# One-hots of a dense scatter moved to ScalarE, value rows respread over the periods, and one expert group instead of two gathered whole

## The chip, the cores and the metric

One core of one Trainium2 chip runs the program. The metric is device time in microseconds for one execution. The kernel before was timed in three runs: median 2061.11, lowest 2057.94, highest 2066.78. A profiled execution is another run, with its own time.

## What is computed

A decoder layer over 256 tokens of width 2048: a mixer (causal pooling and forgetting attention), memory cross-attention, and a product-key expert network. Only the last part matters here. `h` is (256, 2048), heads are 8, keys 128, and 16384 experts have a row `u` and a row `v` of 2048 floats each:

```python
q = (h @ w_query).reshape(B, S, PEER_HEADS, 2, PEER_HALF)
scores = jnp.einsum('bshcd,hckd->bshck', q, sub_keys)
s_top, i_top = lax.top_k(scores, 16)
cand = s_top[..., 0, :, None] + s_top[..., 1, None, :]
cand_idx = i_top[..., 0, :, None] * 128 + i_top[..., 1, None, :]
best, pos = lax.top_k(cand.reshape(..., 256), 16)
expert_idx = take_along_axis(cand_idx.reshape(..., 256), pos)
gate = softmax(best)
act = gelu(einsum('ckd,cd->ck', expert_u[expert_idx], h))
out = einsum('ck,ckd->cd', gate * act, expert_v[expert_idx])
```

Each token picks 16 experts in each of 8 heads, so 128 rows of u and 128 of v. The layer ends with the residual sum and an RMS norm.

## The kernel before, in words

Tokens are two tiles of 128 (c = 0, 1), one token in each partition. A group is one head of one tile: 16 groups, g = 8c + head, each with 16 expert columns k. One gather brings one row for each of the 128 tokens of a tile.

**Routing** (VectorE: `route_keys`, `route_pairs`, `route_experts`, L1165 to L1189) writes the expert numbers `idx` of a group and adds 1 to the semaphore `routed`. `gate_exp` (ScalarE, L723) and `gates` (VectorE, L1194) make its softmax. Group g + 2 is routed inside the period of group g.

**Dots** (VectorE, `dot_products`, L1236 and L1238): two halves of 1024 elements for each u row. The u rows land in seven slots: four in `u_ring`, two in `u_mid`, one in `u_high`; for groups 0 and 1 only the four. GpSimd issues all gathers in one written order (`gather_u` L495, `gather_v` L502): within period p for each k first u row (p, k), which waits until the dot that used its slot is done, then a share of the value rows, each of which waits until TensorE has used its slot (`v_used`). After 16 dots, `sum_dots` (L1200), gelu on ScalarE (L751), and `weights` (L1206, L1207), behind the first two dots of the next group.

**Values** of tile 0: for each of 128 expert columns ScalarE writes a diagonal matrix of weights (`diagonals`, L731, four buffers) and TensorE multiplies it with the value row tile, four matmuls of 512 columns into `misc` (`take_values`, L1664). `v_share(p)` says which of the 128 are taken in period p: 8 in each of periods 2 to 7, 10 in each of 8 to 15.

**Dense part.** Experts whose first key is 80 or more (48 of 128 keys) are not gathered as value rows: such indices lie beyond the gather's bound and are skipped, and their weight in the diagonal is set to zero. Their weights are scattered instead into a matrix wT (128 second keys x 48 first keys x 128 tokens), and after the dots TensorE multiplies 48 tiles of 128 consecutive v rows with it (`dense_tile`, L1697, each tile once for tile 0 into `misc` and once for tile 1 into `acc`). SyncE loads the tiles into three slots of `u_ring` (L432). The last WHOLE = 2 groups (14 and 15) are left out of this: their value rows are gathered whole. The scatter runs by batches of 8 tokens, 16 batches for each tile. `turn_lists` (TensorE, L1682) turns the lists of a tile over, `take_lists` (VectorE, L1214) copies them to `listsT`. For each batch VectorE compares to get `hotA` (second key one-hot, 128 x 8 x 128, L1221) and `hotB` (first key one-hot of 48, L1223, times the weight, L1225); TensorE multiplies them per token (`scatter_weights`, L1691); ScalarE copies the result into wT (`weights_T`, L745). `hotA`, `hotB` and the result have two buffers. `scatters(p)` says which batches go into period p: three in 8 to 12, one in 13, for tile 0; eight in 14 and eight in 15 for tile 1. TensorE and ScalarE go through a period in ten steps, a value and then its batches; VectorE has the batches in front of dots 2 to 15.

**Late values** of tile 1: 128 more gathers into seven slots (`late_landed`); VectorE adds them weighted into `y_sum` (`add_values`, L1270, 2048 elements), except that of the last 16 every second goes to TensorE (`late_diagonal` L738, `take_late` L1673). `finish(0)` stands on VectorE before addition 112 and waits for the low half of the dense tiles; `finish(1)` (L1279 to L1292) ends the program.

The start of the layer takes the first 740 us and is not touched. The periods run from about 812 (the end of group 0's dots) to 1666, dense tiles and late values from there to the end.

```python
for p in range(1, GROUPS):
    pool.wait_ge(routed, p + 1)
    share = v_share(p)
    for k in range(TOP):
        gather_u(p, k)
        for n in share[k * len(share) // TOP:(k + 1) * len(share) // TOP]:
            ...
            gather_v(n, n % VS, v_landed[n % VS])
```

## Time and profile before

| | |
|---|---|
| median of three runs | 2061.11 us |
| the profiled execution's own time | 2061.64 us |
| its span | 2059.6 us |
| mean granted TensorE clock | 0.952 of full speed |
| TensorE matmul busy | 1773.1 us (86%) |
| VectorE busy | 1402.9 us (68%) |
| ScalarE busy | 447.8 us (22%) |
| GpSimd busy | 1027.9 us (50%) |
| HBM read | 729.91 MB |

The shares are means over stages with different limits: in the first 740 us TensorE is nearly always busy, in the periods DMA and VectorE are. So the page is only the start, and the trace is asked by stretches of time. A busy figure for GpSimd here is the time it takes to issue gathers. PEclk is the clock granted to TensorE as a share of 2.4 GHz; 0.5 is its lower level, 1.2 GHz.

### The profile page before, as it was taken

How to read it: one execution, taken by the hardware profiler on the slowest of the kernel's cores; microseconds unless marked ns; L12 is line 12 of the kernel's file. 1: busy time of each engine (PE TensorE's matmuls, PEld its weight loads, DVE VectorE, ACT ScalarE, POOL GpSimd, SP SyncE). 2: the span in 40 equal slices, each digit the busy share in tenths (PEclk: the TensorE clock that was granted, in tenths of full speed). 3: DMA queues.
4: the chain of work that ended last, by engine and by line, in shares of the span. 5: the costliest groups of instructions: out<-in, count | busy, mean ns of one | idle time of the engine just before them, and what ended most of it. 6: DMA issues, size and time to landing. Idle time of an engine off the chain costs nothing.

```text
span 2059.6 us, 21224 instructions
## 1 busy us (share of the span) xinstructions
PE 1773.1 (86%) x7539; PEld 1184.9 (58%) x7539; DVE 1402.9 (68%) x2235; ACT 447.8 (22%) x720; POOL 1027.9 (50%) x643
## 2 busy tenths in 40 slices
PE   7999999999999999466565667877778899999996
PEld 7998998888998898322222223333334544444442
DVE  4382453233333258899888888999989877887865
ACT  5344453345434410201101101111101100000001
POOL 4443343444332313456556546554556756776742
PEclk9999999999999999789999889988889999999999
DMA  8975455655535689899999999999999989999997
GB/s 207 245 172 137 152 181 159 196 191 185 165 122 190 198 313 396 316 408 420 420 419 419 414 390 388 401 389 393 394 419 402 377 323 403 387 405 371 395 421 290
DMA packets 157648, 647.40 MB, mean 314 GB/s; under 512 B 25894, under 2 KB 31086, under 8 KB 95598
## 3 DMA queue, kind: packets, MB, share of 16 engines
q0 software_dynamic: 73728, 450.98, 54.2%
q1 hardware_dynamic: 83824, 195.16, 29.5%
q8 instruction: 58, 0.95, 0.2%
q14 instruction: 38, 0.31, 0.0%
HBM read 729.91 MB, written 2.10 MB: 355 GB/s over the span
## 4 chain that ended last, share of the span: by engine, by line
PE 47%; DMA 19%; DVE 18%; issue 8%; POOL 6%; ACT 1%; DVEq 0%; SPq 0%; POOLq 0%; ACTq 0%
PE misc L1664 10%; DMA u_ring<-in_peer_u_dram,idx 7%; DMA v_low<-in_peer_v_dram,idx 6%; DVE product L1236 6%; DVE product L1238 5%; PE acc L1355 5%; PE acc L1357 5%; PE acc L1356 5%; PE acc L1362 5%; PE acc L1363 5%; PE acc L1364 5%; PE acc L1691 2%; DMA v_more<-in_peer_v_dram,idx 2%; DMA v_last<-in_peer_v_dram,idx 2%; DMA v_high<-in_peer_v_dram,idx 2%
## 5 line engine op out<-in xcount | busy, mean ns | idle before, releaser
L455 POOL TENSOR_TENSOR w_lo<-raw,w_hi 128x1024 fp32r<-128x1024 f32 x112 | 273.7, 2444 | 428.9 <-ACT w_hi L543 428.6
L1664 PE MATMUL misc<-v_low,diag 128*128 128x512 f32 x512 | 263.5, 667 | 132.7 <-ACT diag L731 87.9
L1664 PE MATMUL misc<-v_high,diag 128*128 128x512 f32 x512 | 263.2, 666 | 108.4 <-DMA v_high<-in_peer_v_dram,idx 71.4
L834 DVE TENSOR_TENSOR w_lo<-raw,w_hi 128x1024 fp32r<-128x1024 f32 x112 | 150.1, 1341 | 267.6 <-ACT w_hi L543 267.3
L543 ACT ACTIVATE w_hi<-raw 128x1024 fp32r<-128x1024 f32 x224 | 237.0, 1060 | 352.4 <-PE acc L1364 169.2
L495 POOL DMA_INDIRECT u_ring<-in_peer_u_dram,idx x160 | 207.3, 1296 | 202.2 <-DVE dots L1238 139.6
L1664 PEld LDWEIGHTS misc<-v_low,diag 128*128 128x128 f32 x512 | 105.7, 214 | 278.2 <-issue 207.3
L1355 PE MATMUL acc<-t_hi,w_hi 128*128 128x256 f32 x896 | 255.3, 285 | 0.0
L1357 PE MATMUL acc<-t_hi,w_lo 128*128 128x256 f32 x896 | 253.5, 283 | 0.0
L1356 PE MATMUL acc<-t_lo,w_hi 128*128 128x256 f32 x896 | 253.5, 283 | 0.0
L1664 PEld LDWEIGHTS misc<-v_high,diag 128*128 128x128 f32 x512 | 104.6, 212 | 253.6 <-issue 157.2
L1236 DVE CUSTOM_DVE_ANT_0 product<-u_ring,hn 128x1024 bf16<-128x1024 f32 x160 | 196.0, 1225 | 51.9 <-DMA u_ring<-in_peer_u_dram,idx 36.0
L502 POOL DMA_INDIRECT v_low<-in_peer_v_dram,idx x102 | 156.5, 1535 | 135.1 <-PE misc L1664 74.7
L502 POOL DMA_INDIRECT v_high<-in_peer_v_dram,idx x100 | 152.0, 1520 | 122.1 <-PE misc L1664 85.4
L1238 DVE CUSTOM_DVE_ANT_0 product<-u_ring,hn 128x1024 bf16<-128x1024 f32 x160 | 195.7, 1223 | 0.0
L1697 PE MATMUL misc<-u_ring,wT 128*128 128x512 f32 x384 | 174.4, 598 | 4.1 <-DMA u_ring<-in_peer_v_dram 3.5
L1362 PE MATMUL acc<-w_hi,t_hi 128*128 128x512 f32 x448 | 177.3, 396 | 0.0
L1364 PE MATMUL acc<-w_hi,t_lo 128*128 128x512 f32 x448 | 174.5, 389 | 0.0
L1363 PE MATMUL acc<-w_lo,t_hi 128*128 128x512 f32 x448 | 174.4, 389 | 0.0
L1697 PE MATMUL acc<-u_ring,wT 128*128 128x512 f32 x384 | 172.3, 592 | 0.0
L1355 PEld LDWEIGHTS acc<-t_hi,w_hi 128*128 128x128 f32 x896 | 171.9, 192 | 0.2
L1356 PEld LDWEIGHTS acc<-t_lo,w_hi 128*128 128x128 f32 x896 | 171.9, 192 | 0.1
(248 smaller groups left out, 2571.9 us busy)
## 6 DMA issues: line engine op xcount, KB each, us to landing
u_ring<-in_peer_v_dram SPq DMA_DIRECT2D x48, 1024.0 KB, 8.9
raw<-in_w_in_dram SPq DMA_DIRECT2D x64, 512.0 KB, 5.1
raw<-in_xattn_wk_dram SPq DMA_DIRECT2D x32, 512.0 KB, 4.6
raw<-in_xattn_wv_dram SPq DMA_DIRECT2D x32, 512.0 KB, 4.0
raw<-in_w_out_dram SPq DMA_DIRECT2D x32, 512.0 KB, 4.6
raw<-in_xattn_wq_dram SPq DMA_DIRECT2D x32, 512.0 KB, 4.6
raw<-in_xattn_wo_dram SPq DMA_DIRECT2D x32, 512.0 KB, 4.8
praw<-in_peer_wq_dram SPq DMA_DIRECT2D x32, 512.0 KB, 8.5
```

The lines of the kernel that those rows point to most:

```text
L455: nc.gpsimd.tensor_tensor(w_lo[:, j % RING, :, :], raw[:, j % RING, :, :], w_hi[:, j % RING, :, :].bitcast(F32), ALU.subtract).then_inc(lo ...
L502: nc.gpsimd.indirect_dma_start(out=v_slot(slot), out_offset=None, in_=v_rows, in_offset=bass.IndirectOffsetOnAxis(ap=idx[:, n // TOP, n % ...
L1236: nc.vector.tensor_tensor_reduce(out=product[:, 0:D // 2], in0=u_slot(n)[:, 0:D // 2], in1=hn[:, c, 0:D // 2], scale=1.0, scalar=0.0, op0= ...
L1238: nc.vector.tensor_tensor_reduce(out=product[:, D // 2:], in0=u_slot(n)[:, D // 2:], in1=hn[:, c, D // 2:], scale=1.0, scalar=0.0, op0=ALU ...
L1355: nc.tensor.matmul(o, wh, hi[:, kt, :], start=first and ct % 2 == 0, stop=False, skip_group_check=True)
L1356: nc.tensor.matmul(o, wh, lo[:, kt, :], start=False, stop=False, skip_group_check=True)
L1357: ins = nc.tensor.matmul(o, wl, hi[:, kt, :], start=False, stop=last and ct % 2 == 1, skip_group_check=True)
L1362: nc.tensor.matmul(o, xh, w_hi[:, s, kk, :], start=first, stop=False)
L1363: nc.tensor.matmul(o, xh, w_lo[:, s, kk, :], start=False, stop=False)
L1364: ins = nc.tensor.matmul(o, xl, w_hi[:, s, kk, :], start=False, stop=last)
L1664: ins = nc.tensor.matmul(o, diag[:, n % 4, :], v_slot(n % VS)[:, i * CW:(i + 1) * CW], start=False, stop=False)
L1697: ins = nc.tensor.matmul(o, wT[c][:, t, :], u_ring[:, t % 3, i * CW:(i + 1) * CW], start=c == 1 and t == 0, stop=c == 0 and t == DENSE - 1)
```

## The change

WHOLE becomes 1, so group 14 takes part in the dense scatter too and only group 15 is gathered whole; all 16 batches of tile 1 then stand in period 15, since group 14's weights are known only there. Twelve of them (and all sixteen of tile 0) get `hotA` from ScalarE: the square of (second key - column) for 8 tokens in turn, then one relu of 1 - 2x over all; every fourth batch of tile 1 (b % 4 == 3) keeps VectorE's comparison. `hotB` stays on VectorE. Value rows are taken 4 in period 1, 6 in each of periods 2 to 7, 11 in each of 8 to 15. Batches of tile 0 stand at k = 8, 11 and 14. TensorE and ScalarE walk a period in 16 steps, as VectorE does. Routing is one period ahead instead of two. The u slots from group 2 on begin with the three outside `u_ring`, the late value slots with the three outside v_low and v_high. `weights(15)` stands behind three late additions.

```diff
-    WHOLE = 2
+    WHOLE = 1
...
-            return n % 4 if n < 2 * TOP else (n - 2 * TOP) % 7
+            return n % 4 if n < 2 * TOP else (n - 2 * TOP + 4) % 7
...
-        def scatters(p):
+        def scatters(p, k):
+            if p < PH or k < 2:
+                return range(0)
+            if p < GROUPS - WHOLE:
+                b = 3 * (p - PH) + (k - 8) // 3
+                return range(b, b + 1) if k in (8, 11, 14) and b < BATCHES else range(0)
+            return range(BATCHES + (k - 2) * BATCHES // 14, BATCHES + (k - 1) * BATCHES // 14)
+        def by_dve(b):
+            return b >= BATCHES and b % 4 == 3
...
+        FIRST_V = 4
         def v_share(p):
             if p < 2:
-                return range(0)
-            return range(8 * (p - 2), 8 * (p - 1)) if p < PH else range(48 + 10 * (p - PH), 58 + 10 * (p - PH))
+                return range(0, FIRST_V * p)
+            if p < PH:
+                return range(FIRST_V + 6 * (p - 2), FIRST_V + 6 * (p - 1))
+            at = FIRST_V + 6 * (PH - 2) + 11 * (p - PH)
+            return range(at, min(at + 11, TILE0))
+        def taken(p, k):
+            n = len(v_share(p))
+            return n if k >= TOP else sum(TOP * i + n < k * n for i in range(n))
+        def late_slot(m):
+            return (m + 4) % V2S
...
+            def key_one_hots(b):
+                t, q, rows = b % BATCHES * WB, b % 2, HS if b < BATCHES else HS - WHOLE * TOP
+                act.wait_ge(lists_copied, b // BATCHES + 1)
+                if b >= 2:
+                    act.wait_ge(wT_done, b - 1)
+                for i in range(WB):
+                    ins = nc.scalar.activation(hotA[0:rows, q, i, :], keys[0:rows, :], ACT.Square, scale=-1.0,
+                                               bias=listsT[0:rows, 1, t + i:t + i + 1])
+                ins.then_inc(key_squares, 1)
+                act.wait_ge(key_squares, act_batches(b + 1))
+                nc.scalar.activation(hotA[0:rows, q, :, :], hotA[0:rows, q, :, :], ACT.Relu, scale=-2.0, bias=1.0).then_inc(key_hot, 1)
...
             def period(p):
...
+                for k in range(TOP):
+                    diagonals(share[taken(p, k):taken(p, k + 1)])
+                    if k == 2 and p in (PH, GROUPS - WHOLE):
+                        key_one_hots(0 if p == PH else BATCHES)
+                    if k == 5 and p + 1 < GROUPS:
+                        gate_exp(p + 1)
+                    for b in scatters(p, k):
+                        if (b + 1) % BATCHES and not by_dve(b + 1):
+                            key_one_hots(b + 1)
                         weights_T(b)
                 gelu(p, p % 2, p // PH)
...
                 dve.wait_ge(lists_done, c + 1)
+                if c:
+                    dve.wait_ge(key_hot, BATCHES)
+                    dve.wait_ge(hot_ready, BATCHES)
...
             def one_hots(b):
+                dve.wait_ge(lists_copied, b // BATCHES + 1)
+                if by_dve(b):
+                    nc.vector.tensor_tensor(hotA[0:rows, q, :, :], ...)
...
             def period(g):
                 dot_products(g, q, c, range(0, 2))
                 weights(g - 1)
-                    route_keys(g + 2)
+                    route_keys(g + 1)
                 for k in range(2, TOP):
+                    for b in scatters(g, k):
                         one_hots(b)
                     dot_products(g, q, c, range(k, k + 1))
+                    if k == 3 and more:
+                        route_pairs(g + 1)
                     if k == 5 and more:
+                        route_experts(g + 1)
+                    if k == 9 and more:
+                        gates(g + 1)
                 sum_dots(g, q)
...
-            dot_products(1, 1, 0, range(8, AHEAD))
+            dot_products(1, 1, 0, range(8, 9))
             dve.wait_ge(scores_ready, 2)
-            route(2)
+            route_keys(2)
+            dot_products(1, 1, 0, range(9, 11))
+            route_pairs(2)
+            dot_products(1, 1, 0, range(11, 13))
+            route_experts(2)
+            dot_products(1, 1, 0, range(13, 15))
             gates(2)
-            dot_products(1, 1, 0, range(AHEAD, TOP))
+            dot_products(1, 1, 0, range(15, TOP))
             sum_dots(1, 1)
-            route(3)
-            gates(3)
...
-            weights(GROUPS - 1)
             for m in range(TILE0):
+                if m == 3:
+                    weights(GROUPS - 1)
...
             def scatter_weights(b):
                 pe.wait_ge(hot_ready, b + 1)
+                if not by_dve(b):
+                    pe.wait_ge(key_hot, act_batches(b + 1))
...
+            for n in v_share(1):
+                take_values(n)
             for p in range(2, GROUPS):
...
+                for k in range(TOP):
+                    for n in share[taken(p, k):taken(p, k + 1)]:
                         take_values(n)
+                    for b in scatters(p, k):
                         scatter_weights(b)
```

GpSimd's issue order changes in the same way: after the u rows of group 1 it issues the four values of `v_share(1)`, then goes on as before with `late_slot`.

## Rows read from the trace of the kernel before

**Rows 1.** Windows by period: busy us (instructions), granted clock, DMA share, GB/s

```profile
926.40:976.70 50.30, 32.18 (x64) 13.10 (x64) 46.77 (x102) 5.61 (x13) 30.91 (x25) 0.90 1.02 420
976.70:1194.20 217.50, 131.01 (x250) 50.37 (x250) 187.22 (x410) 22.76 (x52) 125.89 (x97) 0.93 1.01 418
1194.20:1542.30 348.10, 270.14 (x724) 129.03 (x723) 315.46 (x661) 42.95 (x104) 181.72 (x154) 0.88 0.98 396
1542.30:1603.10 60.80, 52.42 (x192) 30.13 (x191) 55.80 (x93) 7.63 (x18) 43.56 (x25) 0.89 1.00 402
1603.10:1666.10 63.00, 55.12 (x216) 32.21 (x214) 55.25 (x92) 7.01 (x19) 37.54 (x23) 0.95 0.96 383
1666.10:1999.60 333.50, 328.41 (x784) 146.89 (x783) 257.86 (x113) 3.53 (x8) 227.80 (x114) 0.99 0.97 385
```

**Rows 2.** The DMA queues: packets, MB, share of 16 engines

```profile
q0 software_dynamic: 73728, 450.98, 54.2%
```

**Rows 3.** Timeline of VectorE: start, us, instruction

```profile
865.74 0.17 DVE L1200 TENSOR_TENSOR dot_sums<-dots 128x16 f32<-128x16 f32 x1
...
876.15 1.23 DVE L1236 CUSTOM_DVE_ANT_0 product<-u_ring,hn 128x1024 bf16<-128x1024 f32 x1
...
999.25 1.23 DVE L1236 CUSTOM_DVE_ANT_0 product<-u_ring,hn 128x1024 bf16<-128x1024 f32 x1 [0.26 <-DVE pos L1160]
...
1001.77 1.23 DVE L1236 CUSTOM_DVE_ANT_0 product<-u_mid,hn 128x1024 bf16<-128x1024 f32 x1
```

**Rows 4.** Groups of instructions, 1200 to 1680: busy, mean ns, idle before

```profile
L1221 DVE TENSOR_TENSOR hotA<-listsT,keys 128x1024 f32<-128x1024 f32 x16 | 19.5, 1221 | 0.7
...
L1223 DVE TENSOR_TENSOR hotB<-listsT,keys 128x384 f32<-128x384 f32 x16 | 8.8, 550 | 0.0
```

**Rows 5.** The window from 860, and TensorE's first values in its timeline

```profile
860.00:880.00 20.00, 6.00 (x8) 2.59 (x9) 17.86 (x53) 3.16 (x8) 11.26 (x11) 0.52 0.95 373
...
874.00 6.32 PE L1664 MATMUL misc<-v_low,diag 128*128 128x512 f32 x8 [28.88 <-ACT diag L731]
```

**Rows 6.** Groups of ScalarE, whole run (busy, mean ns, idle before), and its timeline

```profile
L543 ACT ACTIVATE w_hi<-raw 128x1024 fp32r<-128x1024 f32 x224 | 237.0, 1060 | 352.4 <-PE acc L1364 169.2 <-PE acc L1357 159.9 <-DMA raw<-in_w_in_dram 15.3
...
L751 ACT ACT_TABLE_LOAD x14 | 18.0, 1283 | 0.2
...
L768 ACT ACTIVATE junk<-y_sum 128x512 bf16<-128x512 f32 x8 | 4.9, 618 | 349.8 <-DVE y_sum L1279 329.6 <-DVE y_sum L1281 20.2
...
1492.13 1.26 ACT L731 ACTIVATE diag<-ident,low_wts 128x128 f32<-128x128 f32 x4
```

**Rows 7.** Timeline of TensorE, then of ScalarE: one step of period 14

```profile
1562.57 3.67 PE L1664 MATMUL misc<-v_high,diag 128*128 128x512 f32 x8 [0.96 <-ACT diag L731]
...
1568.92 5.31 PE L1664 MATMUL misc<-v_high,diag 128*128 128x512 f32 x8 [0.96 <-ACT diag L731]
...
1567.99 0.49 ACT L745 ACTIVATE wT<-acc 128x384 f32<-128x384 f32 x1 [5.57 <-PE acc L1691]
1568.38 0.39 ACT L731 ACTIVATE diag<-ident,low_wts 128x128 f32<-128x128 f32 x1
```

**Rows 8.** Timeline of TensorE: first and last dense tiles

```profile
1674.60 3.70 PE L1697 MATMUL misc<-u_ring,wT 128*128 128x512 f32 x8 [0.58 <-ACT wT L745]
...
1994.28 5.40 PE L1697 MATMUL misc<-u_ring,wT 128*128 128x512 f32 x8 [3.55 <-DMA u_ring<-in_peer_v_dram]
```

**Rows 9.** Timeline of TensorE, then of VectorE: the tail

```profile
2045.57 3.70 PE L1673 MATMUL acc<-v_low,diag 128*128 128x512 f32 x8 [1.21 <-DMA v_low<-in_peer_v_dram,idx]
...
2049.38 2.48 DVE L1281 TENSOR_TENSOR y_sum<-acc,y_sum 128x512 f32<-128x512 f32 x4 [3.94 <-PE acc L1673]
```

**Rows 10.** Timeline of VectorE, then waits from 1542 to 1680

```profile
1550.81 0.56 DVE L1214 COPY listsT<-acc 96x384 f32<-96x384 f32 x1 [0.97 <-PE acc L1682]
...
1674.77 0.17 DVE L1206 TENSOR_TENSOR lists<-acts,gate 128x16 f32<-128x16 f32 x1 [8.53 <-ACT acts L751]
...
POOL v_low L502 <- PE misc L1664: 20.6, 5, 8.1
```

More of the change, by code:

```diff
@@ L298, in hybrid_layer @@
         PC = CH * ITEMS["peer"][1]
-        AHEAD = 12
         TILE0 = PH * TOP
@@ L490, in gather_u @@
                 before = u_before(n)
-                if before is None:
+                if before is not None:
+                    pool.wait_ge(dot_done, before + 1)
+                elif n >= 2 * TOP:
                     pool.wait_ge(scores_ready, ITEMS["peer"][1])
-                elif before >= 0:
-                    pool.wait_ge(dot_done, before + 1)
                 nc.gpsimd.indirect_dma_start(
@@ L511, in _, with first_values @@
                 gather_u(0, k)
-            for p in range(1, GROUPS):
+            def first_values(n):
+                if n >= VS:
+                    pool.wait_ge(v_used, n - VS + 1)
+                elif n == 2:
+                    pool.wait_ge(peer_used, PC - CH)
+                gather_v(n, n % VS, v_landed[n % VS])
+            pool.wait_ge(routed, 2)
+            for k in range(TOP):
+                gather_u(1, k)
+            for n in v_share(1):
+                first_values(n)
+            for p in range(2, GROUPS):
                 pool.wait_ge(routed, p + 1)
@@ L753, in period @@
             def period(p):
-                share, turns = v_share(p), scatters(p)
-                for i in range(10):
-                    diagonals(share[i:i + 1])
-                    if i == 3 and p + 2 < GROUPS:
-                        gate_exp(p + 2)
-                    for b in turns[i * len(turns) // 10:(i + 1) * len(turns) // 10]:
+                share = v_share(p)
+                for k in range(TOP):
[7 more added lines that the diff above has]
+                            key_one_hots(b + 1)
                         weights_T(b)
@@ L1701, in _ @@
                 nc.tensor.matmul(o, zeros[:, 0:P], zeros[:, :], start=True, stop=False)
+            for n in v_share(1):
+                take_values(n)
             for p in range(2, GROUPS):
-                share, turns = v_share(p), scatters(p)
+                share = v_share(p)
                 if p == PH:
@@ L1707, in _ @@
                     turn_lists(1)
-                for i in range(10):
-                    for n in share[i:i + 1]:
+                for k in range(TOP):
+                    for n in share[taken(p, k):taken(p, k + 1)]:
                         take_values(n)
-                    for b in turns[i * len(turns) // 10:(i + 1) * len(turns) // 10]:
+                    for b in scatters(p, k):
                         scatter_weights(b)
```

61 lines of the change are left out of this document (22 added, 39 removed).

## The prediction

> **What bounds the kernel now.** Read the windows by period first, a period being the dots of one of the 16 groups [rows 1]. The DMA share is 1.02 in period 3 and 1.01 in periods 4 to 7, at 420 and 418 GB/s, and 0.98 at 396 GB/s in periods 8 to 13. The queues [rows 2] tell how much a gather moves. One whole gather is 128 rows of 8 KB, 1.0486 MB; the indirect queue moved 450.98 MB, which is 430.1 of them. 256 are u rows and 32 are whole value rows (groups 14 and 15), so the other 224 value gathers, whose high keys are skipped, are worth 142.1, or 0.634 each. The sum below uses that.
>
> Then VectorE. A dot comes every 2.52 us (999.25 to 1001.77), 40.4 us in a group [rows 3]. Period 3 (50.3 us, DMA fed it) shows dots and one routing with nothing else: VectorE's floor without one-hots is 50.3. A batch of one-hots adds hotA 1.22 and hotB twice 0.55 [rows 4], so periods 8 to 13 with three batches have a VectorE floor of 50.3 + 3 x 2.32 = 57.3; they take 348.1 / 6 = 58.0 [rows 1]. Their bytes are 16 + 10 x 0.634 = 22.3 gathers, 23.4 MB, 55.8 us at 0.419 MB per us. So VectorE bounds these. Periods 3 to 7 need (16 + 8 x 0.634) x 1.0486 / 0.419 = 52.7 us for bytes and take (50.3 + 217.5) / 5 = 53.6: DMA bounds them.
>
> After the last dot, TensorE bounds. The 48 dense tiles start at 1674.60, when the last batch's copy is in, and the low half of the sums is complete with the record of 1994.28, at about 1999.5. That stretch of 325 holds 93 half tiles, one DMA wait of 3.55 and one record 1.8 longer than its like: 319.6 / 93 = 3.44 us for a half tile, without gaps [rows 8]. DMA is at 0.97 beside that [rows 1]: it is nearly a second bound. In the tail TensorE waits for each late value row (1.21 for the last), its sums are taken up at 2049.38, and the output is done 10.2 later [rows 9].
>
> **The change, part by part.**
> (1) Start of period 2. Before, groups 2 and 3 are both routed before it: group 1's dots are summed at 865.74, and the first dot of group 2 starts at 876.15 [rows 3]. After, group 3 is routed inside period 2. The same work moves, it doesn't vanish; what vanishes is the 10.3 us between them in which no dot runs, and four early values and gathers into three free slots use the DMA there. The first u gather of group 2 goes out behind 13 of group 1's dots and the routing, three dots or 7.6 us before the period starts; two u rows and the four values, 4.5 gathers or 11 us of DMA, were issued in the six us before it. So I let the first dot wait some 2 us: 868. Period 2 then ends at 868 + 50.3 + 1 = 919.3 against 926.4: -7.
> (2) Periods 3 to 7 carry 6 values, not 8: 19.8 gathers, 20.8 MB, 49.6 us. VectorE's 50.3 takes over. With half a us of jitter 50.8 each: 5 x (50.8 - 53.6) = -14.
> (3) Periods 8 to 14. In 8 to 12 three hotA leave VectorE (-3.66, floor 53.6); 13 has one batch, 14 none. Eleven values make 22.97 gathers, 24.1 MB, 57.4 us. DMA is the bound in all seven; at 57.8 each 404.6 against 348.1 + 60.8 = 408.9: -4. The value rows that periods 2 to 7 no longer carry are paid here. All 128 still land before the end of period 15, so no bytes are saved up to there.
> So group 15's dots start at 1603.1 - 25 = 1578.
> (4) Period 15 is where the change pays. Its sixteen batches were eight, beside ten values; now eleven values. ScalarE makes twelve wide one-hots: eight squares of 128 columns and a relu over 1024. Neither is in the trace. The diagonal has the same shape and a column operand: 0.39, four in 1.26, so eight take 0.39 + 7 x 0.29 = 2.4; a pass over 1024 takes 1.06 at w_hi [rows 6]. Called K: 2.4 + 1.06 + two handovers of 0.1 = 3.7. Ends: 3.5 with nothing between, 6.1 if a square and a relu each cost a table load of 1.28 ([rows 6]; the squares of L768 need none behind a sqrt).
> The Trainium skill, page "ScalarE: Activation LUTs", section "Rules for kernel authors", says to put relu, add and multiply on VectorE, which speaks against this move. Instruction by instruction the rows agree, 1.22 against about 3.7. Whether that shows hangs on the chain that follows (rival F takes it as it stands).
> That chain runs through TensorE and ScalarE in program order. TensorE does value (3.67), batch (6.35 - 3.67 - 0.95 = 1.73); ScalarE copies the batch (0.39 until it takes the next, 0.49 until done), makes the next diagonal (0.39), and TensorE starts again 0.95 after the batch: 1562.57, 1568.92, a step of 6.35 [rows 7]. The new order puts the next batch's K ahead of this batch's copy. With a value between batches K hides beside it (3.7 against 5.4). Where two batches follow one another without a value, ScalarE stands: copy 0.5, K 3.7, copy 0.5, diagonal and handover 0.4: 5.1 instead of 0.95. From the loop bounds: values at k = 1, 2, 3, 5, 6, 8, 9, 11, 12, 14, 15; batches one at each k from 2 to 15, two at 8 and at 15. From the copied lists on: TensorE's second value and the first batch, with two K on ScalarE beside them (7.4), 8.4; nine value+batch, 9 x 5.4 = 48.6; handovers 4 x 0.95 + one double without K 2.7 + 4 x 5.1 = 26.9; last batch and copy 2.3. Sum 86. The granted clock is 0.88 to 0.95 in periods 8 to 15 [rows 1], and a value at the low level costs 5.31 instead of 3.67 [rows 7]: +5. The lists are copied 8 us after the period's start (1542.3 to 1551.4 in period 14, with a gelu wait of 1.3 that goes [rows 10]). Together 8 + 86 + 5 = 99; dense tiles start at 1578 + 99 = 1677, +2.5 against now. VectorE has 40.4 + 16 x 1.10 + 4 x 1.22 = 63 to do and waits for TensorE; DMA needs 57 and idles. What four periods' rearrangement won is given back in one.
> (5) Dense tiles. Group 14's value rows shrink by 16 x 0.366 x 1.0486 = 6.1 MB, 16 us at the 385 GB/s of that stretch [rows 1]. TensorE's 320 stays, and the stall of 3.55 plus 1.8 goes: end of the low half at 1677 + 320 = 1997 (-2.6).
> (6) Tail. All seven slots can hold landed rows when the low half ends, so the eight late values go at TensorE's pace: three high tiles 10.3, then 8 x 3.6, 39 us, against 49.8 (1999.5 to 2049.3 [rows 9]): -10.7. The queue still gives the last two gathers 33 to 36 us after the low half, inside 39. Behind it 10.3 as now.
> (7) weights(15) moves behind three additions: VectorE's 8.53 us wait [rows 10] is filled. VectorE has 112 x 2.46 = 276 us of additions under TensorE's 320, so this costs or gives nothing while that cover holds.
> Sum on the profiled execution: 1997 + 39 + 10.3 = 2046.3 in a span of 2059.6, -13.3; I take -11, since (3) and (4) have more ways to lose a microsecond than to win one. Its own time is 2061.64, the median of the three runs 2061.11: **2050**.
>
> **The rivals.**
> A, forecast: (1) to (6) as they stand, -18 to -6. Chance 0.42.
> B, period 15 is shorter: K overlaps more than I let it, or fewer slow stretches. If the four doubles cost 2.7 as the one without K does, 10 us go, without the +5 of the clock 15, and some more from (3) if DMA holds 420. End -20 to -35, 2027 to 2042. For it: ScalarE is busy for only 43 us of 348 in periods 8 to 13 [rows 1]. Against: order, not load, makes those waits. Chance 0.2.
> C, slower: TensorE's clock in period 15. When TensorE waits, the granted clock falls to its lower level: 0.52 from 860 to 880 behind 28.88 us of idleness [rows 5], and eight records took 6.32, not 3.67. Period 15 has nine waits, TensorE busy some 75%. If the clock is low for more than half of the stretch, each value costs 2.65 and each batch 1.7 more: 11 x 2.65 + 16 x 1.7 = 56 in full; at 60% 34, of which 5 is counted: end -11 + 29 = +18, 2080. It decides from a mean clock of about 0.75 in period 15 on. Against it: 0.95 in the same mixture now. With it goes K at its upper end, 4 x 2.4 = 10 in the doubles and some beside values, about +5 in the end. Chance 0.15.
> D, the periods give nothing: ScalarE's and TensorE's order stalls POOL, as TensorE's values hold it back now (20.6 us for v_low alone, 1542 to 1680) [rows 10], and u gathers queue behind it. Periods 8 to 14 then take 59.5, +12 against (3): end 2062. Chance 0.12.
> E, the smaller gathers do not show, because dense tiles and tail are TensorE's already: (5) and (6) give nothing; +2.5 of (4) alone, 2064. Against it: the waits for DMA in rows 9. Chance 0.06.
> F, K is hidden nowhere: all twelve lengthen period 15 by 3.7 - 1.22 = 2.5, 30 us, where the chain above counts 4 x (5.1 - 0.95) = 17. End +13 on the forecast, 2063. Against it: in the step of 6.35 ScalarE works 0.9 and waits 5.57 [rows 7]. The skill's rule named in (4) would have it so. Chance 0.05.
>
> **Numbers.** A measurement of this kernel tells 0.5%, 10.3 us, from no change: faster is below 2050.8. A lies 0.24 below and 0.18 above that, B below; D, E and F inside but for 0.02 of D that stalls more; C above 2071.4. Faster 0.44, same 0.39, slower 0.17. Range: B without its last few us (0.06 left out) to C's near end (0.12 left out), 2030 to 2074.
>
> **What would show it.** Period 2 starts before 870; periods 3 to 7 at 50.5 to 51.5; 8 to 14 at 57 to 58.5 with DMA at 1.0; group 15's dots start at 1573 to 1585; period 15 lasts about 90 with DMA share near 0.7; K at 3.5 to 3.8 with no table load; dense tiles start within 5 us of 1677, without a DMA wait; TensorE's late values back to back. Wrong if period 15's chain lasts under 80 or over 105, or if dense tiles wait for DMA.

## The result and the profile after

The changed kernel takes **2075.0 us** (median of 6 runs, 2072.25 to 2077.07) against 2060.45 for the kernel before (6 runs): ratio 1.0069, interval 1.0056 to 1.0083. It is slower by 0.7%, where the prediction had 2050 and faster. Its profiled execution has a span of 2070.2 us at a mean granted clock of 0.947; it is the fastest of the six, so the profiles below differ by 10.6 us where the medians differ by 14.5.

Windows of the changed kernel, columns as in [rows 1]: periods 3 to 7 with half of 2, periods 8 to 13, period 14, period 15, the dense tiles to the end of the low half, the tail.

```profile
919.00:1173.30 254.30, 145.07 (x242) 56.21 (x241) 233.93 (x510) 25.13 (x55) 150.00 (x112) 0.83 1.01 416
1173.30:1526.90 353.60, 285.94 (x786) 134.58 (x785) 297.04 (x645) 101.74 (x256) 187.55 (x160) 0.94 1.00 406
1526.90:1588.10 61.20, 44.97 (x90) 18.07 (x89) 46.82 (x104) 7.09 (x16) 32.43 (x28) 0.92 1.00 405
1588.10:1689.10 101.00, 79.71 (x325) 48.28 (x324) 59.98 (x105) 50.69 (x134) 24.15 (x21) 0.86 0.61 233
1693.50:2017.90 324.40, 322.48 (x745) 142.84 (x746) 263.62 (x114) 2.36 (x5) 245.35 (x116) 0.99 0.99 389
2017.90:2060.00 42.10, 38.61 (x89) 16.19 (x87) 24.25 (x18) 6.10 (x16) 15.29 (x11) 1.00 0.85 338
```

Against [rows 1]: up to period 7 the change wins 20.9 us (1194.2 to 1173.3). Periods 8 to 13 give 5.5 back (353.6 for 348.1): DMA was at 0.98 there and is at 1.00 now. Period 15 takes 101.0 instead of 63.0, with TensorE busy 79.7 of them, ScalarE 50.7 and DMA at 0.61: no engine is full, so much of the time lies in waits between engines.

VectorE at the start of period 2: the sum of group 1's dots, then the first dot of group 2, against [rows 3].

```profile
863.09 0.17 DVE L1243 TENSOR_TENSOR dot_sums<-dots 128x16 f32<-128x16 f32 x1
867.90 1.23 DVE L1284 CUSTOM_DVE_ANT_0 product<-u_mid,hn 128x1024 bf16<-128x1024 f32 x1 [4.64 <-DMA u_mid<-in_peer_u_dram,idx]
```

TensorE in period 15, then ScalarE in the same stretch, against [rows 7]. The first line is a value whose row landed late; the last line of the first fence is TensorE's total wait for diagonals from 1588 to 1694 (us in total, times, longest).

```profile
1606.05 5.40 PE L1715 MATMUL misc<-v_high,diag 128*128 128x512 f32 x8 [1.74 <-DMA v_high<-in_peer_v_dram,idx]
...
1625.77 3.67 PE L1744 MATMUL acc<-hotB,hotA 112*128 112x48 f32 x32
1632.41 6.22 PE L1715 MATMUL misc<-v_high,diag 128*128 128x512 f32 x8 [2.97 <-ACT diag L757]
1638.46 3.67 PE L1744 MATMUL acc<-hotB,hotA 112*128 112x48 f32 x32
1645.11 6.69 PE L1715 MATMUL misc<-v_high,diag 128*128 128x512 f32 x8 [2.97 <-ACT diag L757]
...
PE misc L1715 <- ACT diag L757: 15.7, 8, 3.0
```

```profile
1640.38 0.49 ACT L771 ACTIVATE wT<-acc 128x384 f32<-128x384 f32 x1 [8.12 <-PE acc L1744]
1640.77 2.43 ACT L781 ACTIVATE hotA<-keys,listsT 112x128 f32<-112x128 f32 x8
1643.24 1.06 ACT L785 ACTIVATE hotA<-hotA 112x1024 f32<-112x1024 f32 x1
1644.20 0.47 ACT L771 ACTIVATE wT<-acc 128x384 f32<-128x384 f32 x1
1644.57 0.39 ACT L757 ACTIVATE diag<-ident,low_wts 128x128 f32<-128x128 f32 x1
```

Read the two fences together. TensorE has done two batches by 1642.1 and wants the next diagonal. ScalarE has stood 8.12 us behind TensorE's value and batch; then it does copy, one-hot, copy and only then the diagonal, which is there at about 1645. TensorE's value that follows takes 6.69 us where 3.67 is usual. The clock goes with it; windows of 20 us in period 15:

```profile
1620.00:1640.00 20.00, 16.07 (x75) 10.46 (x74) 10.20 (x17) 8.71 (x23) 7.31 (x6) 0.83 0.67 254
1640.00:1660.00 20.00, 14.06 (x62) 9.10 (x61) 13.10 (x22) 12.48 (x33) 2.46 (x3) 0.78 0.36 116
1660.00:1680.00 20.00, 16.07 (x68) 9.99 (x67) 9.33 (x18) 12.10 (x32) 0.00 (x0) 0.84 0.45 157
```

Groups of ScalarE in period 15 (columns as in [rows 6]): the wide one-hot itself, without a table load between.

```profile
L781 ACT ACTIVATE hotA<-keys,listsT 112x128 f32<-112x128 f32 x96 | 29.2, 388 | 7.0 <-DVE listsT L1260 7.0
L785 ACT ACTIVATE hotA<-hotA 112x1024 f32<-112x1024 f32 x12 | 12.7, 1056 | 0.4
```

TensorE at the first dense tile, the last low one, and two late values; then VectorE's last sum ([rows 8], [rows 9]).

```profile
1693.54 6.39 PE L1750 MATMUL misc<-u_ring,wT 128*128 128x512 f32 x8 [0.58 <-ACT wT L771]
...
2014.24 3.70 PE L1750 MATMUL misc<-u_ring,wT 128*128 128x512 f32 x8 [1.88 <-DMA u_ring<-in_peer_v_dram]
...
2051.24 3.70 PE L1724 MATMUL acc<-v_high,diag 128*128 128x512 f32 x8 [1.28 <-DMA v_high<-in_peer_v_dram,idx]
```

```profile
2059.99 2.48 DVE L1328 TENSOR_TENSOR y_sum<-acc,y_sum 128x512 f32<-128x512 f32 x4 [3.93 <-PE acc L1724]
```

### The profile page after: what moved, and what is told of

It reads as the page before. It is cut to its first block, busy times and chain, and to the rows that moved or that the text cites. A ratio compares the mean times of both kernels' runs of the same rounds, so it can differ in the third digit from the quotient of the medians.

```text
span 2070.2 us, 21509 instructions
## 1 busy us (share of the span) xinstructions
PE 1795.9 (87%) x7539; PEld 1193.2 (58%) x7539; DVE 1371.2 (66%) x2207; ACT 546.4 (26%) x974; POOL 1019.9 (49%) x643
## 3 DMA queue, kind: packets, MB, share of 16 engines
q0 software_dynamic: 73728, 444.89, 53.2%
## 4 chain that ended last, share of the span: by engine, by line
PE 59%; DMA 20%; DVE 14%; issue 4%; POOL 2%; ACT 1%; DVEq 0%; POOLq 0%; SPq 0%; ACTq 0%
PE acc L1750 8%; DMA v_high<-in_peer_v_dram,idx 8%; PE misc L1750 8%; PE misc L1715 7%; PE acc L1406 5%; PE acc L1407 5%; PE acc L1408 5%; DVE product L1284 5%; PE acc L1413 5%; PE acc L1415 5%; PE acc L1414 5%; DMA u_ring<-in_peer_u_dram,idx 5%; DVE product L1286 5%; DMA v_low<-in_peer_v_dram,idx 4%; PE acc L1744 1%
## 5 line engine op out<-in xcount | busy, mean ns | idle before, releaser
L1715 PE MATMUL misc<-v_high,diag 128*128 128x512 f32 x512 | 280.9, 701 | 123.1 <-DMA v_high<-in_peer_v_dram,idx 103.9
L1715 PEld LDWEIGHTS misc<-v_high,diag 128*128 128x128 f32 x512 | 109.7, 225 | 284.4 <-DMA v_high<-in_peer_v_dram,idx 145.4
L1284 DVE CUSTOM_DVE_ANT_0 product<-u_ring,hn 128x1024 bf16<-128x1024 f32 x160 | 196.1, 1226 | 67.1 <-DMA u_ring<-in_peer_u_dram,idx 52.1
L519 POOL DMA_INDIRECT v_high<-in_peer_v_dram,idx x100 | 146.3, 1463 | 141.3 <-PE misc L1715 109.4
L519 POOL DMA_INDIRECT v_low<-in_peer_v_dram,idx x100 | 145.0, 1450 | 114.5 <-PE misc L1715 74.6
```

Of the source, the lines that this page charges most:

```text
L519: nc.gpsimd.indirect_dma_start(out=v_slot(slot), out_offset=None, in_=v_rows, in_offset=bass.IndirectOffsetOnAxis(ap=idx[:, n // TOP, n % ...
L1284: nc.vector.tensor_tensor_reduce(out=product[:, 0:D // 2], in0=u_slot(n)[:, 0:D // 2], in1=hn[:, c, 0:D // 2], scale=1.0, scalar=0.0, op0= ...
L1715: ins = nc.tensor.matmul(o, diag[:, n % 4, :], v_slot(n % VS)[:, i * CW:(i + 1) * CW], start=False, stop=False)
```

## The experiments

One table from the timelines of all kernels, in us. "To 7" is the end of period 7; "15 on" the stretch from the sum of group 14's dots (the start of group 15's) to the first dense tile. Each ratio is against runs of the kernel before on the same chip.

```
kernel       to 7    8-14   15 on  dense at  span    median   ratio, interval
before       1194.2  408.9  71.5   1674.6    2059.6  2060.45
changed      1173.3  414.8  105.4  1693.5    2070.2  2075.00  1.0069 1.0056-1.0083
whole2       1175.5  420.5  78.0   1674.0    2052.7  2055.63  0.9967 0.9950-0.9984
dve15        1173.1  414.9  91.3   1679.3    2056.1  2061.70  0.9996 0.9982-1.0010
warm         1175.3  415.4  94.8   1685.5    2062.0  2065.33  1.0010 0.9997-1.0024
spread12     1174.3  428.5  91.7   1694.5    2072.6  2078.29  1.0072 1.0049-1.0095
alldve       1173.5  415.1  91.2   1679.8    2056.9  2062.01  0.9993 0.9981-1.0005
early        1172.9  415.7  104.4  1693.0    2071.1  2074.31  1.0057 1.0040-1.0074
diag         1175.3  415.3  79.3   1669.9    2048.2  2053.84  0.9958 0.9941-0.9974
best1        1175.5  414.9  91.4   1681.8    2058.5  2062.54  1.0000 0.9989-1.0012
before_diag  1191.1  404.1  74.2   1669.5    2052.8  2055.14  0.9974 0.9963-0.9985
diag_w2      1174.5  415.4  73.9   1663.9    2046.0  2049.58  0.9947 0.9930-0.9963
diag_wfront  1176.3  415.3  82.7   1674.3    2055.1  2053.74  0.9964 0.9954-0.9974
diag_ring5   1174.5  417.7  82.8   1675.0    2052.3  2053.28  0.9960 0.9946-0.9974
v10          1176.8  400.7  103.4  1681.0    2062.3  2062.26  1.0006 0.9997-1.0016
even         1187.4  404.6  75.2   1667.2    2049.5  2051.05  0.9954 0.9938-0.9971
```

**whole2**: everything of the change but its first line, group 14 stays whole.

```diff
-    WHOLE = 1
+    WHOLE = 2
...
-            return range(BATCHES + (k - 2) * BATCHES // 14, BATCHES + (k - 1) * BATCHES // 14)
+            per = BATCHES // WHOLE
+            at = BATCHES + per * (p - GROUPS + WHOLE)
+            return range(at + (k - 2) * per // 14, at + (k - 1) * per // 14)
```

> The changed kernel with groups 14 and 15 both gathered whole and the batches of tile 1 spread over periods 14 and 15, eight each; all else stays. Theory 1 (the crowded period 15 is the loss, the other parts won): periods 14 and 15 take 58 to 61 us each, DMA stays above 0.95 in both, the dense tiles start 20 us earlier than in the kernel before (near 1655 instead of 1693), and the whole is about 20 us faster than before, near 2040. Rival (the respread values and the routing one ahead are the loss, and group 14's bytes are worth their 16 us): the dense tiles start near 1680 and the end is later than the changed kernel's, near 2085.

Neither expectation came: the dense tiles start at 1674.0, between 1655 and 1680, and periods 14 and 15 take 66.9 and 67.7 where 58 to 61 were said. The kernel takes 19 us less than the changed one: "15 on" falls from 105.4 to 78.0, while period 14 takes its share of batches and comes to 66.9. From the first dense tile to the end of the low half it needs 325.2, and 43.3 for the tail, against 324.4 and 42.1, with all of group 14's bytes in it. So gathering group 14 with skipped rows buys some 2 us from the first dense tile on, and what costs is that all sixteen batches of tile 1 then stand in one period.

**dve15, alldve**: who makes the wide one-hots, in period 15 and everywhere.

```diff
-            return b >= BATCHES and b % 4 == 3
+            return b >= BATCHES
...
-                    if k == 2 and p in (PH, GROUPS - WHOLE):
+                    if k == 2 and p in (PH, GROUPS - WHOLE) and not by_dve(0 if p == PH else BATCHES):
```

> The changed kernel with all sixteen wide one-hots of tile 1 made by VectorE, none by ScalarE in period 15. Theory 1 (the wide one-hots on ScalarE stand between TensorE's batch and its next value): the four waits of 2.97 us in period 15 fall to about 1, period 15 to dense tiles 105 -> 95, the whole 8 to 12 us less than the changed kernel, near 2063. Rival (sixteen batches and eleven values beside one group are too much, whoever makes the one-hots; VectorE's 78 us and TensorE's order are the floor): 102 or more, the whole within 4 us of the changed kernel.

In alldve the first line is `return True`.

> The changed kernel with all 32 wide one-hots on VectorE, as before the change; respread values, routing one ahead and one whole group stay. Beside the run with only tile 1's on VectorE (dense tiles at 1679.3, group 15's dots from 1588.0) this tells what ScalarE's share is worth in periods 8 to 12. Theory of the prediction (VectorE had to be relieved there): periods 8 to 12 take 3.66 us more each where VectorE is the bound, floor 57.3, so about 0 to +8 in all, end 2061 to 2070. Rival (nothing there hangs on who makes them, or ScalarE's make TensorE wait): group 15's dots from 1588 or before, end 2061 or less.

With VectorE's one-hots in period 15 the stretch is 14.1 us shorter and TensorE's waits are 0.96 each again. Doing the same in 8 to 14 changes nothing: 415.1 against 414.9, though VectorE then works 361.6 us there instead of 343.9. In the changed kernel VectorE doesn't set these periods.

**warm**: idle matmuls on TensorE in period 15, nothing else.

```diff
+                    if p == GROUPS - 1 and k >= 2:
+                        for i in range(12 if k in (7, 8, 10, 13) else 3):
+                            nc.tensor.matmul(acc[:, 1, 1, :], zeros[:, 0:P], zeros[:, :], start=True, stop=True)
```

> The changed kernel with idle bf16 matmuls into an unused bank behind TensorE's batches of period 15: twelve where it waits 2.97 us, three where it waits 0.96. Theory: the values there took 5.4, 6.2, 6.7, 6.3 and 6.3 instead of 3.67 because the granted clock fell in those waits (window clocks 0.78 to 0.84); with the idle work the clock stays near 1.0, the values near 3.7, period 15 to dense tiles 105 -> 95 and the whole near 2063. Rival (the clock falls whatever fills the waits, or filling them delays what follows): clock as before, the whole 2073 to 2080.

Its windows of the same stretch as above, and one value behind a pair of batches:

```profile
1620.00:1640.00 20.00, 19.69 (x105) 12.62 (x103) 11.85 (x20) 10.10 (x26) 6.37 (x6) 1.00 0.78 302
1640.00:1660.00 20.00, 19.62 (x107) 12.44 (x106) 14.59 (x25) 12.48 (x33) 2.13 (x3) 1.00 0.40 126
```

```profile
1632.09 2.76 PE L1770 MATMUL acc<-zeros 128*128 128x512 bf16 x12
1634.68 3.63 PE L1715 MATMUL misc<-v_high,diag 128*128 128x512 f32 x8
```

The clock is back at 1.00, the value at 3.63, and the stretch is 10.6 us shorter. That is the price of the low clock in the changed kernel; the rest of the loss stays.

**spread12**: twelve values in each of 8 to 14, four left for 15.

```diff
-            at = FIRST_V + 6 * (PH - 2) + 11 * (p - PH)
-            return range(at, min(at + 11, TILE0))
+            at = FIRST_V + 6 * (PH - 2) + 12 * (p - PH)
+            return range(at, min(at + 12, TILE0))
```

> The changed kernel with twelve value rows in each of periods 8 to 14 instead of eleven, which leaves four in period 15. Theory (period 15 is bound by the order of TensorE and ScalarE, periods 8 to 14 by DMA bytes): each of 8 to 14 takes 1.5 us more, +10 in all; period 15 to dense tiles goes from 105 to about 70; the whole near 2050. Rival (in 8 to 14 the value ring and not the bytes sets the pace): the seven periods take 3 us more each, +20, and period 15 gives 30 back: near 2062.

Seven values fewer at 3.67 are 26 us of TensorE's work, yet "15 on" falls only by 13.7, to 91.7 and not to 70. TensorE has less to fill its waits, and the mean clock of the stretch is 0.68; that the waits are the reason was not tested by itself. What is won there, periods 8 to 14 lose: 428.5, 13.7 more, between the 10 of the theory and the 20 of the rival. Both expectations missed the whole, which is 2078.29.

**early**: in 8 to 13 VectorE makes its one-hots two dots ahead of the batch.

```diff
-                    for b in scatters(g, k):
+                    for b in scatters(g, k + 2 if g < GROUPS - WHOLE and k + 2 < TOP else k if g >= GROUPS - WHOLE else 0):
```

> The changed kernel with VectorE's one-hots of tile 0 two dots earlier (before dots 6, 9 and 12; TensorE and ScalarE keep them at 8, 11 and 14). Periods 8 to 14 took 414.8 us where 404.6 were forecast. Theory (TensorE waits at a batch for VectorE's one-hots, VectorE for u rows, and GpSimd's queue, with the u rows in it, for a value that TensorE takes only behind that batch): periods 8 to 12 shrink by 1 to 2 us each, group 15's dots from 1580 to 1584, the whole 5 to 8 us less than the changed kernel. Rival (DMA's bytes at the rate that the periods show, 0.406 MB per us, are the bound): within 2 us of 1588.

Nothing moves (415.7, 104.4). How early VectorE makes its one-hots isn't what holds these periods.

**diag**: ScalarE writes each diagonal one value ahead, so that it no longer stands behind one-hot and copies.

```diff
+                diagonals(share[0:1])
                 for k in range(TOP):
-                    diagonals(share[taken(p, k):taken(p, k + 1)])
+                    diagonals(share[taken(p, k) + 1:taken(p, k + 1) + 1])
```

> The changed kernel with ScalarE making each diagonal one value ahead, so that it stands before the batch's copy and not behind it. Theory (order): in period 15 TensorE no longer waits 0.96 or 2.97 for a diagonal; nine waits of 19.9 us in all fall to what K itself holds back, period 15 to dense tiles 105 -> 93, the whole near 2063; periods 8 to 14 1 us less each at most. Rival (K of the next batch is what TensorE waits for, the diagonal only shows it): a wait for the one-hots takes the diagonal's place and period 15 stays above 101.

TensorE between 1629 and 1640:

```profile
1629.35 3.67 PE L1716 MATMUL misc<-v_high,diag 128*128 128x512 f32 x8
1632.85 3.67 PE L1745 MATMUL acc<-hotB,hotA 112*128 112x48 f32 x32
1636.36 3.67 PE L1716 MATMUL misc<-v_high,diag 128*128 128x512 f32 x8
```

Two lines of code take 26 us off "15 on", more than twice the 12 of the theory. No wait for a diagonal is left in period 15, where the changed kernel has 15.7 us of them, and two values take 5.2 to 5.3 where five took 5.2 to 6.7, though ScalarE makes the same twelve one-hots: most of the loss was what stood behind them. With this the changed kernel is 0.4% faster than the kernel before.

**best1**: dve15, warm and diag together.

> Three of these edits together: tile 1's wide one-hots on VectorE, idle matmuls behind period 15's batches, diagonals one value ahead. If order, clock and diagonals each cost what theory 1 says, period 15 to dense tiles falls from 91.3 (VectorE's one-hots alone) to VectorE's own floor, 8 + 40.4 + 16 x 2.32 = 86 or a little less, since the last dot stands behind the last one-hots: end near 2055, faster than the kernel before by 0.3 to 0.5%. If the rival is right (DVE's floor reached already, or the idle matmuls in the way): 91 or more, 2061.

It isn't the sum: 91.4 against 79.3 with diag alone. TensorE is busy 87.42 of the 91.40 us, and VectorE waits 11.5 for its batches. Where nothing else waits, the idle matmuls of warm (2.75 us for twelve) stand in TensorE's full stream; VectorE's one-hots with the diagonals ahead, but without idle matmuls, were not tried:

```profile
1630.18 2.75 PE L1771 MATMUL acc<-zeros 128*128 128x512 bf16 x12
1632.77 3.60 PE L1716 MATMUL misc<-v_high,diag 128*128 128x512 f32 x8
```

**before_diag**: the same two lines in the kernel before, in its walk of ten steps.

```diff
+                diagonals(share[0:1])
...
-                    diagonals(share[i:i + 1])
+                    diagonals(share[i + 1:i + 2])
```

> The kernel before, whole in everything (two whole groups, VectorE's one-hots), with one edit: in its last two periods the diagonals of a batch are issued one value ahead of the batch's copies on ScalarE. Theory (TensorE's wait of 0.96 us ahead of a value is the hand-over of the diagonal behind the copies, as in the changed kernel): the waits go, periods 14 and 15 lose up to 16 x 0.96 = 15 us between them, at least 7; the dense tiles start 7 to 15 us before 1674.6, and the kernel takes 2045 to 2053 us. Rival (those periods are set by the groups' bytes and the batches' own work, the diagonals are hidden): dense tiles within 3 us of 1674.6, and 2060 us.

The dense tiles start 5.1 us earlier and the kernel wins 0.26%, but not where the theory put it. The edit holds for all periods from 2 on, and periods 8 to 13 are 5.7 us shorter (342.4 for 348.1), while 14 and 15 with what follows take 136.0 in place of 132.3. So taking away the waits of 0.96 in 14 and 15 wins nothing there; another limit stood right behind them. Which one wasn't tested. Periods 8 to 13 of before_diag, then of v10 (below, also ten values), columns as in [rows 1]:

```profile
1191.10:1533.50 342.40, 272.77 (x724) 126.57 (x724) 315.45 (x664) 43.51 (x104) 193.70 (x154) 0.91 0.99 404
1176.80:1519.90 343.10, 272.93 (x737) 128.38 (x736) 296.23 (x646) 100.56 (x250) 196.89 (x156) 0.91 1.00 406
```

**diag_w2**: diag and whole2 together.

> The changed kernel with the diagonals one value ahead and with two whole groups, eight batches beside each. Theory (the order on ScalarE was what made periods 14 and 15 take 67 us each with two whole groups): they fall to about 60 each, the dense tiles start at about 1660 in place of 1674.0, and the kernel takes about 2040 us, less than the 2054 of one whole group with the same order. Rival (period 14 is then set by its bytes and its four extra loads beside eight batches, whatever the order): 14 and 15 take 65 or more each, dense tiles at 1670 or later, 2050 to 2056 us.

The lowest ratio of all, 0.9947 of the kernel before and 25 us under the changed one (even, at 0.9954, lies within its interval). The theory's 60 for periods 14 and 15 wasn't reached (62.7 and 66.9), and the time lies between the theory's and the rival's; dense tiles start at 1663.9, 10 us before whole2's. TensorE in period 15 now waits for values, not for ScalarE:

```profile
1641.48 3.70 PE L1718 MATMUL misc<-v_low,diag 128*128 128x512 f32 x8 [2.25 <-DMA v_low<-in_peer_v_dram,idx]
1645.02 1.88 PE L1747 MATMUL acc<-hotB,hotA 96*128 96x48 f32 x16
1649.30 5.40 PE L1718 MATMUL misc<-v_high,diag 128*128 128x512 f32 x8 [2.40 <-DMA v_high<-in_peer_v_dram,idx]
```

**diag_wfront**: diag with the weights of group 15 ahead of the late additions again.

```diff
+            weights(GROUPS - 1)
...
-                if m == 3:
-                    weights(GROUPS - 1)
```

> The changed kernel with the diagonals one value ahead, and the weights of the last group issued ahead of the last additions on VectorE, as in the kernel before. Theory (the 6 us by which the dense stage is shorter than before come from that move, not from group 14's bytes): the stretch from the first dense tile to the end of the low half goes from 325 back to 329 to 332 us, and the kernel takes 2058 to 2060 us. Rival (the move is worth nothing, the 6 us are the bytes'): 325 us and 2054 us.

The kernel time is diag's (2053.74 and 2053.84). In the profiles the stretch is 327.4 against 325.1, below what the theory wanted. The 331.1 before had been read at VectorE's sum at 2005.70, and there VectorE was behind with its additions; TensorE's own end of the low half lies 325 us after the first dense tile before, in whole2 and in diag alike.

**diag_ring5**: diag with a fifth slot for value rows in periods 1 to 14.

```diff
+    v_fifth = put("v_fifth", [P, D], F32, at_v + 16 * KB)
...
-                if n >= VS:
-                    pool.wait_ge(v_used, n - VS + 1)
+                if v_before(n) is not None:
+                    pool.wait_ge(v_used, v_before(n) + 1)
...
```

> The changed kernel with the diagonals one value ahead, and a fifth slot for value rows while periods 1 to 14 run. Theory (periods 8 to 14 take 415 us and not 404 because GpSimd waits for a free value slot, so that the DMA queues run empty at places): they fall to 403 to 408 us, GpSimd's waits on the values shrink, and the kernel takes 2042 to 2047 us. Rival (those periods are set by the bytes at the rate that the DMA engines reach there, about 0.405 MB per us): within 3 us of 415, and 2054 us.

GpSimd's waits from 1174 to 1592, diag first, then diag_ring5 (columns: who waits for whom, us in total, times, longest).

```profile
POOL v_low L519 <- PE misc L1716: 72.9, 21, 7.8
POOL v_high L519 <- PE misc L1716: 64.8, 28, 6.2
```

```profile
POOL v_high L536 <- PE misc L1733: 42.1, 11, 17.9
POOL u_ring L529 <- DVE dots L1304: 38.7, 28, 3.5
POOL v_low L536 <- PE misc L1733: 26.3, 10, 5.3
```

The waits on values fall from 137.7 to 77.8 us (9.4 of them for the fifth slot) and the waits on u slots grow from 13.1 to 67.1; the periods take 417.7 at a DMA share of 0.97, not less than 415. A longer ring only moves GpSimd's waits: it was not what held the periods.

**v10, even**: diag with ten values in 8 to 14 and 18 in period 15; and diag_w2 with 7 in 2 to 7, 10 in 8 to 14, 12 in 15.

```diff
-            at = FIRST_V + 6 * (PH - 2) + 11 * (p - PH)
-            return range(at, min(at + 11, TILE0))
+            at = FIRST_V + 6 * (PH - 2) + 10 * (p - PH)
+            return range(at, at + 10 if p + 1 < GROUPS else TILE0)
```

> The changed kernel with the diagonals one value ahead, ten values in each of periods 8 to 14 in place of eleven, and 18 in period 15. Theory (a value gather takes 1.8 to 1.9 us of the DMA engines' time, and these periods are their time and nothing else): 8 to 14 take 402 us in place of 415. Period 15 gets seven more values at 3.67, so it and the stretch to the dense tiles grow from 79 to about 105, and the kernel takes about 2066 us. Rival 1 (a value gather costs the 1.59 of its bytes, the rest is a lower rate of the whole stream): 404 us. Rival 2 (something else sets these periods, VectorE or GpSimd's order): 412 or more.

> The kernel with two whole groups and the diagonals one value ahead, with 7 values in each of periods 2 to 7, 10 in each of 8 to 14, and 12 in period 15. Theory (value gathers at 1.8 to 1.9 us each of DMA time): periods 3 to 7 rise from 50.8 to about 52.3 each, 8 to 14 fall by about 13 us in all, the end of period 14 stays within 5 us of 1589.9, and the kernel takes 2045 to 2053 us, the same as with 6 and 11. Rival (DMA keeps 0.419 MB per us with 7 values, so these fit below VectorE's 50.3 + 0.4): periods 3 to 7 stay below 51.3 and the end of period 14 comes 8 us or more earlier, 2040 us.

Seven values less take 14.6 us off periods 8 to 14 (expected 13), and seven values more put 24.1 on period 15. In even, periods 3 to 7 take 262.4 / 5 = 52.5 us (theory 52.3, rival below 51.3). The time follows the number of value gathers; who makes the one-hots, how early, and the ring had moved nothing in the changed kernel. What was moved in that time is in the DMA part of the profile, diag from 1175.3 to 1590.6, then v10 from 1176.8 to 1577.5, then the kernel before in periods 4 to 7:

```profile
DMA packets 27260, 168.07 MB, mean 405 GB/s; under 512 B 6754, under 2 KB 6754, under 8 KB 6754
```

```profile
DMA packets 26171, 162.75 MB, mean 406 GB/s; under 512 B 6313, under 2 KB 6313, under 8 KB 6313
```

```profile
DMA packets 14055, 90.96 MB, mean 418 GB/s; under 512 B 2955, under 2 KB 2955, under 8 KB 2955
```

The queue's 73728 packets ([rows 2]) are 144 for each of 512 gathers, before and after the change alike, though 6.1 MB are gone: a skipped row stays a packet, only a small one. The Trainium skill, page "DMA: Bandwidth & Descriptors", section "Why a DMA increments its semaphore by 16 and not by 1", says that each of 16 engines ends its part with a write to the semaphore; 144 = 128 rows + 16 fits that.

In its window v10 moved 1089 / 144 = 7.6 gathers fewer in 14.6 us less: 1.93 us a gather for 5.32 / 7.6 = 0.70 MB. Going up from the changed kernel's 414.8, spread12 adds 13.7 for seven, 1.96. The prediction had priced a value at 0.665 MB and 0.419 MB per us, 1.59. As an estimate, with 1.9 for a value, and (54.4 - 8 x 1.9) / 16 = 2.45 for a u row, periods of 7, 8, 10, 11 and 12 values come to 52.5, 54.4, 58.2, 60.1 and 62.0; measured are 52.5 (even), 54.4 ([rows 1], 217.5 / 4), 58.0 ([rows 1]) and 57.2 (v10), 59.3 and 61.2. From seven values to twelve that is 8.7 us, 1.74 a value (1.4 from eight to ten, 1.9 from eleven to twelve), and the estimate is 0.8 to 1.0 too high from v10 on. So these slopes put a value at 1.7 to 2.0, not more closely.

## Why the prediction was wrong

Its first gains came: step (1) has period 2 at 918.9 (said 919.3, with the first dot at 867.9 for 868), step (2) 50.9 for each of 3 to 7 (said 50.8).

**Step (3) failed first.** It said DMA at 57.8 a period, 404.6 in all; 414.8 came, +10. The bytes were right (24.1 MB in a period; 168.07 / 7 = 24.0), the rate was not. It took 0.419 MB per us from periods where values are few, and 24.0 MB at the measured 0.405 make the 59.3 that came. It read periods 8 to 13 before as VectorE's, because VectorE's floor of 57.3 came so near the 58.0 (16 batches in six periods make it 56.5 on average; period 13 has one batch, not three). v10 shows what ten values cost once VectorE is relieved: 57.2 a period at a DMA share of 1.00, with VectorE busy 296.2 of 343.1, where the text had 55.8 for their bytes. In the changed kernel alldve rules VectorE out as well: 361.6 us of its work in the same 415. The 348.1 before held something more: with the same work, and a DMA share of 0.99 for 0.98, before_diag takes 342.4, so 5.7 us of it were the order of the diagonals, which the prediction looked for in periods 14 and 15 only. Rival D had the size, 59.5 a period, and the wrong cause: it named GpSimd's stalls, and the queue never ran short behind them (DMA share 1.00 in periods 8 to 14).

**Step (4) had the chain right and the clock too small.** It said 99 from group 15's dots to the dense tiles; 105.4 came. The wide one-hots start 3.44 apart (2.45 for eight squares, 1.06 for the relu; said 3.7). Where two batches stand between two values, TensorE starts again 2.97 after the second, which itself takes 3.67 - 1.88 = 1.79: 4.8 from the end of the first, where the text had 5.1. The one such place without a wide one-hot behind it takes 0.96 + 1.79 = 2.75 (said 2.7). The lists were copied 8.1 us into the period (said 8). The clock is the term that was too small: five values at 5.2 to 6.7 where 3.67 is usual make 12 us, the text had 5 and took 5.31 for a slow one, and warm gets 10.6 back. With 7 us more the 99 become 106; the four double places (-1.4) and the row that landed late at 1606 (1.74 for 0.95) nearly cancel. The window clocks of 0.78 to 0.84 stand near rival C's 0.75, but its 34 us were three times too many, and 0.86 over the period is on the forecast's side of its point. So the sum of (4) missed by 6, nearly all of it the clock. The chain was foreseen but taken as given; diag shows that it was the cause, since one changed order takes the waits and most of the slow records away together.

Rival F fell: twelve one-hots at full price would be 30 us, dve15 gives 14 back and diag 26 while keeping them all. The text set it against 4 x (5.1 - 0.95) = 17 for the chain, but the 5.1 holds the second batch; without it the chain's price is 4 x (5.1 - 2.7) = 10, and the trace has 4 x (2.97 - 0.96) = 8, before the clock. The rule of the Trainium skill cited with it, page "ScalarE: Activation LUTs", section "Rules for kernel authors", puts relu and add on VectorE. The trace agrees for the single instruction, 1.22 against 3.5 us. For the kernel the order mattered more: with VectorE's one-hots and the old order the stretch takes 91.2 (alldve), with ScalarE's and the diagonals ahead 79.3 (diag).

**Steps (5) and (6).** The low half ended 324.4 after the first dense tile where 320 was said: the first record took 6.39 and a stall of 1.88 stayed, half of 3.55. The tail is 42.1, said 39, before 49.8. The last three values still wait 0.85 to 1.28 each for DMA. Between them lie 4.95 us, two whole gathers, 2.1 MB: the tail goes at the pace of DMA. What won the 7.7 us there stays open. In the old order little of it is group 14's bytes: whole2 keeps these and has 43.3. With the diagonals ahead it is the other way round: before_diag has 48.1, diag_w2 46.7 and diag, without the bytes, 43.0. The place of weights(15) isn't it: diag_wfront has 43.3. The order of the late slots wasn't tried alone. This is rival E for the bytes: the 6.1 MB, called 16 us of DMA, are worth 2 us in both stretches together (whole2), 4 with diag's order (371.9 for diag_w2, 368.1 for diag).

**Step (7)** stands: free, as said.

The sum, on the profiled execution: -20.9 up to period 7, +5.9 in 8 to 14, +33.9 to the dense tiles, -0.7 in the low half, -7.7 in the tail, 10.2 behind it in both: +10.5, where the spans of 2070.2 and 2059.6 differ by 10.6. The prediction's own sum of -13.3 missed that by 24: 10 in (3), 6 in (4), 4 in (5), 3 in (6), all to one side; it allowed 2 for all of them. The range ended at 2074; its upper end was rival C's near end alone and did not add several terms that miss together.

What stays open: what a single skipped row costs, since the slope (1.7 to 2.0 us for a value) and the mean rate don't fix it well; what won most of the tail; which limit stands behind the waits in periods 14 and 15 of before_diag; and what holds diag_w2's period 15 at 66.9 once values land late (GpSimd waited 21.6 us for the last dots before the first late gather, with DMA at 0.39 from 1650 to 1664).

## What to carry to other kernels

When work is moved to an idle engine, look first at what stands behind it in that engine's program order: here a 0.39 us diagonal stood behind a 3.4 us one-hot, and issuing it one step ahead gave 26 us back with every one-hot kept and turned +0.7% into -0.4%. Price a transfer by periods that have the same mixture as the one that is to grow, not by the best rate elsewhere, and when an engine's floor and the measured period lie within 1 or 2 us, test whether it is the bound at all. Saved bytes count only in a stretch that waits for them, and a remedy for a wait (idle matmuls) costs once the wait is gone.

## What was unexpected of the hardware

- A gather of 128 rows of 8 KB with 38% skipped ((6754 - 16 x 189) of 77 x 128 rows in diag) takes, by estimate from the slopes over v10, spread12 and even, 1.7 to 2.0 us of full DMA time, where its bytes at 0.419 MB per us would take 1.59; skipped rows stay in the queue as packets under 512 B (744 more in the changed kernel, 6.1 MB fewer).
- TensorE's clock fell to 0.78 in a window in which it was still busy 14.1 of 20 us, and to 0.68 over spread12's period 15, busy 71.0 of 91.7. Before, busy 55.1 of 63.0, it was 0.95 [rows 1].
- Square, relu, copy and the scaled diagonal followed each other on ScalarE without a table load: in the changed kernel none stands between 1571.4, ahead of the gelu at 1588, and 1693.7, behind its last copy, with twelve wide one-hots in between.
